# Attention of two heads at a time in the even and the odd layer of a four-layer network

## The reference, cut to what matters

```python
# even layer, latent queries (context queries: the same, with kc_h and vc_h)
s = jnp.einsum('bhgqd,bhkd->bhgqk', qblk, k_all).astype(jnp.float32) * A_SCALE
p = jax.nn.softmax(s, axis=-1).astype(v_all.dtype)
return jnp.einsum('bhgqk,bhkd->bhgqd', p, v_all)
# odd layer, per grid row
s_loc = jnp.einsum('bhqd,bhiqjd->bhqij', qr, kw).astype(jnp.float32) * C_SCALE + bias.astype(jnp.float32)
s_ctx = jnp.einsum('bhqd,bhkd->bhqk', qr, kc_h).astype(jnp.float32) * C_SCALE
s = jnp.concatenate([s_loc.reshape(B, C_HEADS, GRID_W, n_loc), s_ctx], axis=-1)
p = jax.nn.softmax(s, axis=-1).astype(vw.dtype)
```

## Time and profile before

| what | value |
|---|---|
| median of 3 runs | 2402.57 us (2402.05 to 2404.2) |
| profiled execution, own time | 2403.49 us |
| its span | 2401.3 us |
| mean granted clock of TensorE | 0.942 of full speed |
| PE busy | 2059.7 us, 86% |
| DVE, ACT, POOL busy | 648.8, 441.1, 324.5 us |
| memory read | 582.97 MB |

### The profile page before, as it was taken

One profiled execution on the slowest core, in us unless ns is written; L12 is line 12 of the kernel. 1 busy time (PEld: TensorE's weight loads), 2 busy tenths in 40 slices (PEclk: granted clock), 3 DMA queues, 4 the chain that ended last, 5 costly groups with the idle time before them and its releaser, 6 DMA issues.

```text
span 2401.3 us, 29402 instructions
## 1 busy us (share of the span) xinstructions
PE 2059.7 (86%) x12318; PEld 1178.0 (49%) x12318; DVE 648.8 (27%) x1417; ACT 441.1 (18%) x919; POOL 324.5 (14%) x298
## 2 busy tenths in 40 slices
PE   4999969998988747999969888888749999995898
PEld 3567544443444215455643333333236686782785
DVE  2233241111111133122341111111144140288162
ACT  2145221000000002033421000000021230231041
POOL 1111231000000011010121000000000110128030
PEclk8999979999999978999979999999979999997899
DMA  9236338999999966213638999999764414324221
GB/s 368 87 119 213 152 131 352 424 425 424 425 425 425 423 233 209 80 38 126 248 124 359 425 422 424 425 420 425 320 219 140 142 36 143 138 55 156 72 82 53
DMA packets 139090, 594.70 MB, mean 248 GB/s; under 512 B 19332, under 2 KB 30612, under 8 KB 105024
## 3 DMA queue, kind: packets, MB, share of 16 engines
q1 hardware_dynamic: 113168, 557.86, 58.4%
q10 hardware_dynamic: 19600, 28.33, 3.5%
q0 software_dynamic: 6176, 6.42, 0.8%
HBM read 582.97 MB, written 21.65 MB: 252 GB/s over the span
## 4 chain that ended last, share of the span: by engine, by line
PE 78%; DVE 8%; issue 8%; DMA 3%; ACT 3%; POOL 1%; SPq 0%; POOLq 0%; ACTq 0%; DVEq 0%
PE banks L1244 19%; PE banks L1269 10%; PE banks L2056 7%; PE banks L1221 5%; PE banks L715 4%; PE banks L1638 4%; PE banks L703 3%; PE banks L975 3%; PE banks L2058 3%; PE banks L563 3%; PE banks L1640 2%; PE banks L2394 2%; PE banks L726 2%; PE banks L325 2%; DMA RG<-in_ada_w 1%
## 5 line engine op out<-in xcount | busy, mean ns | idle before, releaser
L1244 PE MATMUL banks<-RG,HT 128*64 128x512 f32 x2112 | 482.3, 610 | 90.1 <-issue 88.0
L1244 PEld LDWEIGHTS banks<-RG,HT 128*64 128x64 f32 x2112 | 173.3, 140 | 386.9 <-issue 383.9
L1253 DVE TENSOR_TENSOR AR<-AR,banks 128x256 f32<-128x256 f32 x66 | 39.7, 602 | 556.5 <-ACT AR L1249 496.0
L1373 POOL DMA_INDIRECT y_rows<-AR x66 | 64.4, 976 | 906.3 <-DVE AR L1273 891.6
L1249 ACT ACTIVATE AR<-banks 128x256 f32<-128x256 f32 x66 | 25.4, 384 | 788.4 <-PE banks L1244 788.4
L2056 PE MATMUL banks<-HT,RG 128*128 128x256 f32 x768 | 166.9, 379 | 0.7 <-ACT HT L443 0.7
L2056 PEld LDWEIGHTS banks<-HT,RG 128*128 128x128 f32 x768 | 145.8, 190 | 22.7 <-issue 2.1
L1221 PE MATMUL banks<-AR 128*128 128x256 bf16 x1152 | 148.6, 277 | 3.4 <-DVE AR L1210 3.4
L1221 PEld LDWEIGHTS banks<-AR 128*128 128x128 bf16 x1152 | 109.3, 99 | 62.4 <-issue 49.0
L1269 PE MATMUL banks<-AR 128*64 128x512 f32 x528 | 120.6, 598 | 2.6 <-DVE AR L1262 2.6
L1269 PE MATMUL banks<-RG,AR 128*64 128x512 f32 x528 | 120.6, 598 | 2.6 <-DVE AR L1262 2.6
(11 more groups left out here) (354 smaller groups left out, 2535.9 us busy)
## 6 DMA issues: line engine op xcount, KB each, us to landing
RG<-in_moe_w SPq DMA_DIRECT2D x165, 2048.0 KB, 19.5
AR<-in_moe_w SPq DMA_DIRECT2D x33, 2048.0 KB, 22.0
RG<-in_ada_w SPq DMA_DIRECT2D x24, 2048.0 KB, 8.2
RG<-in_attn_w_in SPq DMA_DIRECT2D x20, 2048.0 KB, 7.9
RG<-in_odd_w_in SPq DMA_DIRECT2D x6, 2048.0 KB, 16.6
RG<-in_ssm_w_in SPq DMA_DIRECT2D x4, 2048.0 KB, 8.0
AR<-y_rows ACTq DMA_DIRECT2D x6, 1024.0 KB, 9.9
RG<-in_even_w_in SPq DMA_DIRECT2D x2, 2048.0 KB, 20.2
```

The costliest lines, as they stand in the source:

```text
L1244: m = pe.matmul(p[64 * h:64 * h + 64, :], x[:, k, :], w[:, :, k, 256 * h:256 * h + 256], start=k == 0, stop=k == 7)
L1373: g.indirect_dma_start(y, off, E.Y[b], None, bounds_check=2047, oob_is_err=False).then_inc(*event)
```

## The change

A unit is now a pair of heads (class `Pairs`, 16 units per stage). The scores of the two heads are two matmuls over 64 rows each, one on the upper and one on the lower row half of the array, into two banks (0 and 1, or 2 and 3), straight from the queries: there is no padding and no zeroing. The values of the two heads alternate on the two column halves and fill one bank of 128 partitions (bank 6), copied out at once. Transposes go to banks 4 and 5; ACT copies one head's, DVE the other's. DVE takes the maximum of both heads in one reduction; in the odd stage it does this for the 256 keys without a bias, and `tensor_tensor_reduce` adds the bias and carries the maximum on in one pass per head. ACT takes two exponentials, POOL scales both heads' probabilities. Two other steps stand in each round, one before and one behind the values, from round 0 on; all of them use bank 7, one after the other. In the odd stage POOL's copy `moved` stands behind its tenth pair. The steps' own instructions, the list of weight loads and the dilated layer's attention are as before. `spread_out` gives the event of a spread's read-out.

```diff
+        def ada_steps(l, parts, streams, rowbanks, spreadbanks):
+
+            last = {}
+            done = []
             for x, n in enumerate(parts):
-                before = done[x - len(rowbanks)] if x >= len(rowbanks) else None
-                yield "rows", n, x, rowbanks[x % len(rowbanks)], before, (done[x - 2], streams[-1]) if x >= 2 else None
+                bank = rowbanks[x % len(rowbanks)]
+                yield "rows", n, x, bank, last.get(bank), (done[x - 2], streams[-1]) if x >= 2 else None
+                last[bank] = ("ada_raw", l, n)
                 done.append(n)
                 for s in streams:
-                    c = len(spreads)
-                    before = spreads[c - len(spreadbanks)] if c >= len(spreadbanks) else None
-                    yield "spread", n, x, spreadbanks[c % len(spreadbanks)], before, s
-                    spreads.append((n, s))
+                    bank = spreadbanks[(x * len(streams) + s) % len(spreadbanks)]
+                    yield "spread", n, x, bank, last.get(bank), s
+                    last[bank] = spread_out(l, n, s)
...
-            return ada_steps(range(4, 12), (0, 1) if l == 0 else (0,), (2,), (3,))
+            return ada_steps(l, range(4, 12), (0, 1) if l == 0 else (0,), (7,), (7,))
...
+        def pe_pairs(pe, A, between):
+            N, name = len(A.units), A.name
+            for s in range(N + 3):
+                if s < N:
+                    u = A.units[s]
+                    if s >= 2:
+                        pe.wait_ge(*at("exped", name, s - 2, 1))
+                    for x in range(2):
+                        m = pe.matmul(PS[2 * (s % 2) + x][:, 0:u["n"]], u["q"][x], u["k"][x], start=True, stop=True)
+                    m.then_inc(*ev("scores", name, s))
+                next(between, None)
+                if s >= 3:
+                    i = s - 3
+                    u = A.units[i]
+                    nb = u["n"] // 128
+                    pe.wait_ge(*at("probs_act", name, i))
+                    pe.wait_ge(*at("probs_dve", name, i))
+                    if i:
+                        pe.wait_ge(*at("att_out", name, i - 1))
+                    for j in range(nb):
+                        for x in range(2):
+                            m = pe.matmul(PS[6][64 * x:64 * x + 64, 0:128], u["v"][x][j],
+                                          A.PT[x][:, 128 * j:128 * j + 128], start=j == 0, stop=j == nb - 1)
+                    m.then_inc(*ev("values", name, i))
+                next(between, None)
+                if 0 <= s - 2 < N:
+                    i = s - 2
+                    for x in range(2):
+                        pe.wait_ge(*at("weighed", name, i, x))
+                        for j in range(A.units[i]["n"] // 128):
+                            m = pe.transpose(PS[4 + x][:, 128 * j:128 * j + 128],
+                                             A.PB[x][i % 3][:, 128 * j:128 * j + 128], IDN[:])
+                        m.then_inc(*ev("probs_turned", name, i, x))
...
+        def act_pairs(act, A, between):
+            N, name = len(A.units), A.name
+            for s in range(N + 3):
+                next(between, None)
+                next(between, None)
+                if 0 <= s - 2 < N:
+                    i = s - 2
+                    n = A.units[i]["n"]
+                    act.wait_ge(*at("probs_turned", name, i, 0))
+                    if i:
+                        act.wait_ge(*at("values", name, i - 1))
+                    act.activation(A.PT[0][:, 0:n], PS[4][:, 0:n], ACT.Copy).then_inc(*ev("probs_act", name, i))
+                if s < N:
+                    u = A.units[s]
+                    act.wait_ge(*at("shift", name, s))
+                    for x in range(2):
+                        if s >= 3:
+                            act.wait_ge(*at("probs_turned", name, s - 3, x))
+                        act.activation(A.PB[x][s % 3][:, 0:u["n"]], PS[2 * (s % 2) + x][:, 0:u["n"]], ACT.Exp,
+                                       bias=A.small_of(s, 1)[:, x:x + 1], scale=u["scale"],
+                                       accum_out=A.small_of(s, 2)[:, x:x + 1]).then_inc(*ev("exped", name, s, x))
...
+        def dve_pairs(v, A, between):
+            N, name = len(A.units), A.name
+            for s in range(N + 3):
+                if s < N:
+                    u = A.units[s]
+                    z = PSA[:, 2 * (s % 2):2 * (s % 2) + 2, 0:u["n"]]
+                    top, free_ = A.small_of(s, 0), 0 if u["bias"] is None else u["bias"][0].shape[1]
+                    v.wait_ge(*at("scores", name, s))
+                    if free_ < u["n"]:
+                        vstep(v, v.tensor_reduce(top, z[:, :, free_:], AX, MAX))
+                    if free_:
+                        for x in range(2):
+                            first = top[:, x:x + 1] if free_ < u["n"] else -3.0e38
+                            ins = v.tensor_tensor_reduce(out=z[:, x, 0:free_], in0=z[:, x, 0:free_], in1=u["bias"][x],
+                                                         scale=1.0, scalar=first, op0=ADD, op1=MAX,
+                                                         accum_out=top[:, x:x + 1])
+                        vstep(v, ins)
+                    v.tensor_scalar(A.small_of(s, 1), top, -u["scale"], None, MUL).then_inc(*ev("shift", name, s))
+                if 0 < s <= N:
+                    v.wait_ge(*at("exped", name, s - 1, 1))
+                    v.reciprocal(A.small_of(s - 1, 3), A.small_of(s - 1, 2)).then_inc(*ev("inverse", name, s - 1))
+                next(between, None)
+                if s >= 3:
+                    i = s - 3
+                    v.wait_ge(*at("values", name, i))
+                    v.tensor_copy(A.units[i]["o"], PS[6][:, 0:128]).then_inc(*ev("att_out", name, i))
+                next(between, None)
+                if 0 <= s - 2 < N:
+                    n = A.units[s - 2]["n"]
+                    v.wait_ge(*at("probs_turned", name, s - 2, 1))
+                    v.tensor_copy(A.PT[1][:, 0:n], PS[5][:, 0:n]).then_inc(*ev("probs_dve", name, s - 2))
...
+        def pool_pairs(g, A, between):
+            N, name = len(A.units), A.name
+            for s in range(N):
+                for x in range(2):
+                    p = A.PB[x][s % 3][:, 0:A.units[s]["n"]]
+                    g.wait_ge(*at("inverse", name, s))
+                    g.tensor_scalar(p, p, A.small_of(s, 3)[:, x:x + 1], None, MUL).then_inc(*ev("weighed", name, s, x))
+                next(between, None)
...
-        def dve_attention_zeros(v, A):
-            for p in range(2):
-                for x in A.QZ[p]:
-                    ins = v.memset(x[64 - 64 * p:128 - 64 * p], 0.0)
-            ins.then_inc(*ev("zeros", A.name))
-
-        def pool_pad(g, A, s):
-            u = A.units[s]
-            if "q" not in u:
-                return
-            if s >= 4:
-                g.wait_ge(*at("scores", A.name, s - 4))
-            p0 = u["p0"]
-            g.tensor_copy(A.padded(s)[p0:p0 + 64], u["q"]).then_inc(*ev("padded", A.name, s))
-            g.wait_ge(*at("padded", A.name, s))
...
+        PB0 = [[ar(13 * KK + 512 * (3 * x + i), 512) for i in range(3)] for x in range(2)]
+        PT0 = [ar(16 * KK + 512 * x, 512) for x in range(2)]
+        SM0 = ar(9 * KK + 512, 4, 8)
         units0 = []
         for t in range(4):
             k0, kn = (0, 512) if t < 2 else (256, 256)
-            for h in range(8):
-                p0, kv = 64 * (h % 2), h // 4
+            for j in range(4):
+                kv, own = j // 2, range(k0 // 128, (k0 + kn) // 128)
                 units0.append(dict(
-                    scores=[(0, kn, KT0[:, kv, k0:k0 + kn])], q=QT0[p0:p0 + 64, h // 2, 128 * t:128 * t + 128],
-                    n=kn, scale=0.125, bias=None, p0=p0,
-                    v=[QKV[:, j, 640 + 64 * kv:704 + 64 * kv] for j in range(k0 // 128, (k0 + kn) // 128)],
-                    o=HT[p0:p0 + 64, h // 2, 128 * t:128 * t + 128]))
-        A0 = Attention("even", units0, PB0, PT0, SM0, QZ0)
+                    q=[QT0[64 * x:64 * x + 64, j, 128 * t:128 * t + 128] for x in range(2)],
+                    k=[KT0[64 * x:64 * x + 64, kv, k0:k0 + kn] for x in range(2)], n=kn, scale=0.125, bias=None,
+                    v=[[QKV[:, i, 640 + 64 * kv:704 + 64 * kv] for i in own]] * 2,
+                    o=HT[:, j, 128 * t:128 * t + 128]))
+        A0 = Pairs("even", units0, PB0, PT0, SM0)
...
-            return PS[j] if hf == 0 else PS[2 + j % 2]
+            return PS[j] if hf == 0 else PS[7]
 
         def odd_before(c, hf, j):
             if hf == 0:
                 return ("odd_out", c - 1, 0, j) if c else None
-            if j >= 2:
-                return "odd_out", c, 1, j - 2
-            return ("odd_out", c - 1, 1, j + 2) if c else ("odd_out", 2, 0, j + 2)
+            if j:
+                return "odd_out", c, 1, j - 1
+            return ("odd_out", c - 1, 1, 3) if c else None
...
```

(30 more changed lines are left out.)

92 lines of the change are left out of this document (36 added, 56 removed).

## The result

The changed kernel takes **2365.85 us** (median of 4 runs, 2363.95 to 2368.08); the kernel before took 2402.31 beside it. The ratio of the two is 0.9848 (95% interval 0.9831 to 0.9865): faster by 36.5 us, inside the range of 2336 to 2368, but 21 us above the forecast of 2344.5. In the two profiled executions the span falls from 2401.3 to 2362.1, by 39.2.

What follows compares the result with a forecast made beforehand. PE was taken to bound both attention stages. From the profiled 2403.49 us, 26.2 (even) and 31.9 (odd) came off, giving 2345.4, then 0.9 for the median of the runs: 2344.5, range 2336 to 2368.

Steps and rivals of the forecast that it cites:

- PE bounds both stages; both halves overlap: Both attention stages: PE-bound, a pair's scores 0.95 us and values 1.02 at 512 keys; work falls 24.8 and 31.5 us.
- rival 1: Scores in both stages: row halves don't overlap, only values merge; price 24.1 us, giving 2368.6; chance 0.13.
- A rule against the change: PE's rounds: each extra change of matmul shape costs 0.13 us, at most 4 us in all, taken into the range.
- the new list of losses: PE's time beside its work in both stages: 12.1 us even and 8.7 odd, 1.4 and 0.4 less than before.
- Even start: First three rounds of the even stage: VectorE waits for the gain's load, fourth round starts at 163.6, 7.9 us lost.
- Bank 7, VectorE's spreads, tails: PE's waits: bank 7 0.9 us even, 2.0 odd; VectorE's spreads 2.0 odd; tails 3.3 even, 4.0 odd.
- rival 2: Before each round's transposes: VectorE, ScalarE and POOL chain outlasts the round; 16 us at half a microsecond each, 2361; chance 0.05.
- rival 3: Slots in both stages: every slot waits for bank 7's previous read-out; at 2 us a round 2421, slower; chance 0.03.
- its point of decision: Bank 7 waits in both stages: 38 rounds at 1.53 us each would eat the 58 us saved.
- So the saving passes through: Behind the attention stages: loads stay ahead, expert stages lose nothing of their own, so 26.2 and 31.9 us reach the total.
- my own mechanism: Both attention stages: PE-bound rounds with both overlaps, time 2337 to 2354; chance 0.79.

Runs made afterwards that it cites:

- the rows' 23.9 us: The changed kernel with both score matmuls of a pair on the same row half: the cost of losing that overlap; whole time 2380.38 us.

## Why the prediction was right, and where it was off

- **PE bounds both stages; both halves overlap:** right. The overlaps' prices (0.85 us per pair of scores and 0.87 of values at 512 keys) are the 0.86 that stood in the sum, and the rows' 23.9 us are rival 1's 24.1. Rival 1 is out.
- **A rule against the change:** underestimated, and this is the term of the sum that was mis-sized most. The forecast took each block at its price among its cheapest old neighbours. In the changed kernel (starts in PE's timeline):

```profile
172.25 1.16 PE L341 MATMUL banks<-AR,IDN 128*128 128x128 f32 x8
173.34 1.09 PE L689 MATMUL banks<-AR 128*64 128x128 f32 x16
...
1037.06 7.13 PE L1719 MATMUL banks<-HT,RG 128*128 128x512 f32 x16
1044.12 1.09 PE L689 MATMUL banks<-AR 128*64 128x128 f32 x16
```

  A part takes 6.87 us between blocks of its own tile shape, 6.97 with another shape on one side (values ahead of it) and 7.06 with one on both (scores ahead, values behind); a spread takes 0.89, 1.00 (180.44 to 181.44) and 1.09. So each side costs about 0.1 us.

  The new order doesn't change shape more often (69 times in the odd stage for 79 before, counted in the timelines), but it puts spreads and parts, which stood among their own shape, beside scores and values.

  The round with two modulation slots takes 5.93 us in the even stage (165.26 to 171.19) and 6.09 in the odd one (1092.24 to 1098.33) for 5.72. The forecast's prices add up to 138.1 us of work in the odd stage (68.7 + 22.2 + 16 x 2.95) and 73.6 in the even one (111.87 - 13.5 - 24.8). PE is busy for 144.9, and for 79.6 in the even stage of the kernel with the moved gain, both at clock 1.00: 13 us more in both, where I put none in the sum and 4 in the range. Some 0.8 of it is no change of shape: half a part was taken at 3.44 us and takes 3.62, as it took 3.64 before.

  The earlier trace rows had a warning: in the odd stage before, PE was busy for 175.5 us where the prices give 169.6. I counted the difference, some of it time at the lower clock, among what PE loses, and the new list of losses has only waits. PE's idle time was less than allowed (6.7 us for 8.7 in the odd stage), which hid part of the miss. That most of the 13 us is the change of shape is an account from PE's timeline; no run removed the switches. The Trainium skill ("TensorEngine Tiling (Array Packing)", "Key Properties") has the array drained at a change of mode, and the trace agrees in kind.
- **Even start:** the fourth round began at 165.26, not 163.6. VectorE's wait for the gain was known, but I took it as given; moving it gives 5.3 us.
- **Bank 7, VectorE's spreads, tails:** right within 1 us each. Two groups of the odd stage, the weighing on GpSimd and the fused operation on VectorE:

```profile
L765 POOL TENSOR_SCALAR AR<-AR,SVT 128x512 f32<-128x512 f32 x27 | 41.9, 1563 | 186.1 <-DVE SVT L746 186.1
L739 DVE CUSTOM_DVE_ANT_0 banks<-banks,AR,SVT 128x256 f32<-128x256 f32 x32 | 14.4, 491 | 0.6
```

  The fused operation took 0.49 us, with 0.41 from one start to the next, for the 0.45 taken; the weighing took 1.56 per half. The rounds hide both: no wait before the transposes stands in a round with two slots, so rival 2 is out. So is rival 3: no wait for bank 7 is longer than 0.78 us, and its point of decision was 1.53 us in each round.
- **"So the saving passes through"**: this step failed. I looked at SP's loads alone and forgot the queue that brings PE's own code. Fewer waits moved all later code, and 4.3 us were lost at the gap and 3.5 at the last read-out, 7.8 of the 8.3 that were given back. Of the profiled execution's miss, 10.6 us lie in the stages (58.1 forecast, 47.5 saved) and 8.3 outside them.
- **Luck:** the range of 2336 to 2368 was drawn up to rivals 1 and 2. The time of 2365.85 lies outside the 2337 to 2354 that I gave my own mechanism, and in the range only because of what the rivals added to it.

## What to carry to other kernels

Price a block in its new neighbourhood, with the shapes on both sides of it, not in the old one, and hold the prices against PE's busy time before. An edit that removes instructions moves all later code of that engine; where the program skips much of it, count the code packets in the gap before and after, and let one branch skip everything. When a stage gets shorter and the whole doesn't, line up the starts of the same instructions, counted from the end, to find where the difference shrinks.

## What the runs showed of the hardware

- PE fetches code in packets of 16 KB (108 packets, 1.77 MB in the whole run, queue q8). Running straight on costs mostly nothing (in the odd stage of the changed kernel ten packets came, and PE was idle only in the waits listed above and in the tail); running past the skipped bodies took PE 36.8 us with six packets, 30.5 to 32.0 with five and 7.9 to 8.2 with one, and from one packet to the next it was 3.2 to 7.4 us. The Trainium skill ("Runtime: NRT & Kernel Launch", "Instruction fetch mechanics") says that a taken branch out of the fetched window stalls until its page has come; the trace agrees, and it adds that the number of such stalls hangs on where the bodies lie.
- The same page calls the crossing of a block boundary mostly hidden. In the last read-out it was not: a packet came at 2291.70, and PE stood for 1.94 us and then ran at the lower of its two clocks, 1.2 GHz, for most of the next 3 us (0.53 in the window from 2294 to 2297). It stood in every kernel with pairs whose code was not padded, and one instruction fewer ahead of it moved it by one matmul record. Why there and not at the neighbouring boundaries stays open.
- The granted clock at the odd stage's start was 1.00 in the changed kernel and in the one without column overlap, and 0.66 to 0.83 over ten microseconds in the other kernels with pairs, worth up to 3 us; what decides it no run here tells. This alone makes two kernels differ by more than a 2 us edit can show.
